# Three weight buffers instead of two in the expert blocks of a mixture-of-experts layer

## What is computed

```
g_w, g_idx = lax.top_k(jax.nn.softmax(g_logits, axis=-1), 1)
e_logits = e_logits[jnp.arange(t), g_idx[:, 0]]
e_w, e_idx = lax.top_k(jax.nn.softmax(e_logits, axis=-1), MOE_TOP_K)
...
def expert_block(args):
    xb, e = args
    h = jax.nn.silu(xb @ w_gate[e]) * (xb @ w_up[e])
    return h @ w_down[e]
```

## Time and profile before

| | us |
|---|---|
| median of 3 runs | 4761.02 (4743.81 to 4763.74) |
| profiled execution | 4764.29 |
| its span | 4762.6 |
| instructions executed in it | 56,977 |
| TensorE busy in the span | 3911.8 (82%) |
| VectorE, ScalarE, GpSimd busy | 1642.3, 706.3, 719.7 |
| stage experts, layer 0 | about 2931 to 3481, 32 blocks |
| stage experts, layer 1 | about 4124 to 4706, 34 blocks |

### The profile page before, as it was taken

One profiled execution on the slowest core, in us unless ns is written; L12 is line 12 of the kernel. 1 busy time (PEld: TensorE's weight loads), 2 busy tenths in 40 slices (PEclk: granted clock), 3 DMA queues, 4 the chain that ended last, 5 costly groups with the idle time before them and its releaser, 6 DMA issues. The chain is left out here.

```text
span 4762.6 us, 56977 instructions
## 1 busy us (share of the span) xinstructions
PE 3911.8 (82%) x23207; PEld 2625.4 (55%) x23207; DVE 1642.3 (34%) x3018; ACT 706.3 (15%) x1502; POOL 719.7 (15%) x595
## 2 busy tenths in 40 slices
PE   4989978999898878999899895877749977577773
PEld 2578855784446756864458743444427755344442
DVE  6667735530365653211341512000031143300003
ACT  2211211010222222100211500000010122000000
POOL 1123303330110213420100101000010033100001
PEclk9999978999899988999899896998969977699987
DMA  3221313623121012221221026999932100599995
GB/s 124 64 80 53 111 49 133 212 98 110 39 68 36 2 50 80 84 89 53 67 77 36 1 80 244 392 396 397 393 127 71 53 1 27 232 396 397 399 396 225
DMA packets 242989, 707.37 MB, mean 149 GB/s; under 512 B 22140, under 2 KB 117828, under 8 KB 192100
## 3 DMA queue, kind: packets, MB, share of 16 engines
q1 hardware_dynamic: 223060, 660.99, 37.5%
q10 hardware_dynamic: 15120, 26.76, 1.6%
q0 software_dynamic: 4608, 16.78, 0.9%
HBM read 667.24 MB, written 37.24 MB: 148 GB/s over the span
## 5 line engine op out<-in xcount | busy, mean ns | idle before, releaser
L3037 PE MATMUL experts_pg<-moe_wg,experts_xt 128*64 128x256 f32 x4224 | 529.4, 414 | 142.3 <-DMA moe_wg<-in_moe_w_up 127.8
L3037 PEld LDWEIGHTS experts_pg<-moe_wg,experts_xt 128*64 128x64 f32 x4224 | 334.5, 150 | 320.2 <-issue 178.0
L465 PE MATMUL ffn_out_y<-ffn_out_ring,ffn_h 128*128 128x512 f32 x704 | 308.8, 601 | 20.8 <-DMA ffn_out_ring<-in_ffn_w_out 20.8
L3052 PE MATMUL experts_py<-moe_wd,experts_ht 128*64 128x512 f32 x1056 | 256.4, 629 | 41.6 <-DVE experts_ht L3104 24.2
L86 PE MATMUL att_proj_ps<-att_proj_ring,ut 128*128 128x512 f32 x576 | 250.0, 597 | 15.6 <-DMA att_proj_ring<-in_attn_w_qkv 15.6
L3102 DVE TENSOR_TENSOR experts_h<-experts_hs,experts_pg 128x256 f32<-128x256 f32 x66 | 27.8, 421 | 659.2 <-ACT experts_hs L3071 659.2
L465 PEld LDWEIGHTS ffn_out_y<-ffn_out_ring,ffn_h 128*128 128x128 f32 x704 | 135.3, 193 | 190.5 <-issue 169.0
L562 PE MATMUL ffn_in_seven<-ffn_in_seven_t,ffn_in_seven_s 128*128 128x256 f32 x1056 | 238.4, 383 | 0.0
L86 PEld LDWEIGHTS att_proj_ps<-att_proj_ring,ut 128*128 128x128 f32 x576 | 177.5, 308 | 87.8 <-DMA att_proj_ring<-in_attn_w_qkv 16.0
L562 PEld LDWEIGHTS ffn_in_seven<-ffn_in_seven_t,ffn_in_seven_s 128*128 128x128 f32 x1056 | 204.0, 193 | 29.1
L562 PE MATMUL ffn_in_seven<-ut,ffn_in_ring 128*128 128x256 f32 x704 | 181.8, 404 | 19.1 <-DMA ffn_in_ring<-in_ffn_w_in 19.1
(11 more groups left out here) (651 smaller groups left out, 6294.0 us busy)
## 6 DMA issues: line engine op xcount, KB each, us to landing
moe_wg<-in_moe_w_gate SPq DMA_DIRECT2D x66, 2048.0 KB, 20.6
moe_wg<-in_moe_w_up SPq DMA_DIRECT2D x66, 2048.0 KB, 25.2
moe_wd<-in_moe_w_down SPq DMA_DIRECT2D x66, 2048.0 KB, 26.2
ffn_in_ring<-in_ffn_w_in SPq DMA_DIRECT2D x44, 1024.0 KB, 5.8
ffn_in_ada_ring<-in_ada_w SPq DMA_DIRECT2D x28, 1024.0 KB, 7.6
ffn_out_ring<-in_ffn_w_out SPq DMA_DIRECT2D x22, 1024.0 KB, 5.0
ssd_proj_ring<-in_ssd_w_in SPq DMA_DIRECT2D x20, 1024.0 KB, 5.3
att_proj_ring<-in_attn_w_qkv SPq DMA_DIRECT2D x9, 2048.0 KB, 7.9
```

Source lines behind the costliest of these rows:

```text
L465: last = nc.tensor.matmul(y[:, tt, half, :], h[:, kk, tt * P:(tt + 1) * P], ring[:, n % RING, q, half * BANK:(half + 1) * BANK], start=(kk ...
L3037: last = nc.tensor.matmul(pg[ch * SLOTS:(ch + 1) * SLOTS, b, side, 0:HH], xt[:, b, kk % MQ, kk // MQ, :], wg[:, b, side, kk, ch * HH:(ch + ...
L3052: last = nc.tensor.matmul(py[half * SLOTS:(half + 1) * SLOTS, b, :], ht[:, b, kk % HM, kk // HM, :], wd[:, b, kk, half * HALF:(half + 1) * ...
```

## The change

The weight buffers, and with them the buffers of a block's rows (`xg`), become three, taken by block modulo 3. They live in a stage of their own, `weights`, which encloses `route` and `experts` and ends before `merge`. `route` issues the weights of three blocks. In `experts` the first 30 blocks (PLAIN) are written out on every engine; only blocks from 30 on run in the loop over pairs, which takes buffers 0 and 1 and waits for block i-2 as before. In the written-out part a load waits for block n-3, and the expert is a constant, since block n of the first 32 belongs to expert n. The rows of blocks 0, 1 and 2 are issued by ScalarE at the beginning of `experts`, those of block 3 on by SyncE ahead of the same block's weights. Results, hidden values and PSUM stay in two buffers.

The diff without the lines that only gained indentation:

```
+WSLOTS, PLAIN = 3, FIRST - 2
...
-        wg, wd = outer.sb("wg", [P, 2, 2, DK, HID]), outer.sb("wd", [P, 2, HK, D])
-        gu_in, d_in = ([outer.sem(f"{n}{b}") for b in range(2)] for n in ("gu_in", "d_in"))
+        weights = Stage(nc, f"moe_w{l}")
+        wg, wd = weights.sb("wg", [P, WSLOTS, 2, DK, HID]), weights.sb("wd", [P, WSLOTS, HK, D])
+        gu_in, d_in = ([weights.sem(f"{n}{b}") for b in range(WSLOTS)] for n in ("gu_in", "d_in"))
...
+        with weights:
...
-                    for b in range(2):
+                        for b in range(WSLOTS):
                             load_gate_up(sp, slice(b, b + 1), b)
                             load_down(sp, slice(b, b + 1), b)
...
-            xg, yb = st.sb("xg", [P, 2, HALF]), st.sb("yb", [P, 2, HALF])
+                xg, yb = st.sb("xg", [P, WSLOTS, HALF]), st.sb("yb", [P, 2, HALF])
...
+                        for n in range(WSLOTS, PLAIN):
+                            load_rows(n, n % WSLOTS, n - WSLOTS + 1)
+                            sp.wait_ge(s["gu_made"], n - WSLOTS + 1)
+                            load_gate_up(sp, slice(n, n + 1), n % WSLOTS)
+                            sp.wait_ge(s["y_made"], n - WSLOTS + 1)
+                            load_down(sp, slice(n, n + 1), n % WSLOTS)
+                        with sp.Fori(PLAIN // 2, more + 1) as it:
+                            for b in range(2):
+                                i = 2 * it + b
+                                e = sp.value_load(info[0:1, bass.ds(i, 1)], min_val=0, max_val=E - 1)
+                                load_rows(i, b, i - 1)
                                 sp.wait_ge(s["gu_made"], i - 1)
                                 load_gate_up(sp, bass.ds(e, 1), b)
                                 sp.wait_ge(s["y_made"], i - 1)
                                 load_down(sp, bass.ds(e, 1), b)
...
-                    one(0, 0, 0, True)
-
-                    one(1, 1, 0, True)
-                    with pe.Fori(1, more + 1) as it:
+                        for n in range(PLAIN):
+                            one(n, n % 2, n % WSLOTS, n // WSLOTS, n < 2)
+                        with pe.Fori(PLAIN // 2, more + 1) as it:
                             for b in range(2):
-                            one(2 * it + b, b, it)
+                                one(2 * it + b, b, b, it - PLAIN // 2 + PLAIN // WSLOTS)
...
+                        for n in range(WSLOTS):
+                            r0 = act.value_load(info[0:1, n + B:n + B + 1], min_val=0, max_val=ASSIGN + SLOTS)
+                            for half in range(2):
+                                act.dma_start(xg[half * SLOTS:(half + 1) * SLOTS, n, :],
+                                              x_rows[bass.ds(r0, SLOTS), half * HALF:(half + 1) * HALF]).then_inc(x_in[n], 16)
```

512 lines of the change are left out of this document (252 added, 260 removed).

## The result

The change makes the kernel slower by a quarter of a per cent: 4770.16 us median of 20 runs against 4757.1, ratio 1.0025, 95% interval 1.0013 to 1.0037, so 6 to 18 us. The prediction was 4756, with no change that can be told. Its own bound for "no change" holds, its sign and its range do not.

A forecast was written before the change was run, and what follows sets the result against it. It took DMA bandwidth to bound the experts stage. Per layer -15.8 - 0.7 + 12.0 + 0.4 + 1.6 = -2.5 us, -5 us for two, gave 4756 us; the 8-in-10 range was 4732 to 4768.

The forecast's parts named there:

- bound for "no change": Whole kernel: a measurement tells about 0.5% (23.8 us) from no change; chance of staying within, 0.80.
- the bound: Experts stage: DMA bandwidth limits it, not late issue; engines' share 1.01 in both layers, 17.4 us a block.
- the scatter: End of route: sharing engines with the prefetch, it and all behind it come 12 us late a layer; bounds 0 to 12.9.
- the third block: Weights prefetched in route: takes off 15.8 us plus 0.7 us of rows, 16.5 us a layer.
- rival 1: Route: the scatter is served first and ends on time; 14.5 us gained a layer, 4732 us; chance 0.12.
- rival 3: DMA streams: mixed HBM reads and writes disturb each other, 3 us more a layer, 4762 us; chance 0.06.
- The extra stage: The new weights stage: one more semaphore clearing and one more barrier, 0.4 us a layer.
- Rows from ScalarE at nothing: Start of experts: issuing rows of blocks 0 to 2 from ScalarE costs nothing, at most 1.3 us a layer late.
- the written-out code: Experts: 6400 more instructions, 0.4 MB a layer of instruction traffic, cost 1.6 us a layer; lower bound 0.
- rival 2: Experts: TensorE starves for instruction pages at 7.3 us each, 139 us a layer partly hidden, near 4950 us; chance 0.06.
- the forecast's upper edge: Whole kernel: top of 4748 to 4761 us, given for a scatter late by 8 to 13 us; chance 0.66.
- none, the share is 1.01, so no reserve: Experts: engines already at full rate, so deeper buffers only fill idle time; pace stays 17.4 us a block.

The follow-up runs named there:

- after: The changed kernel as first measured and profiled, against the kernel before: 4770.16 us, ratio 1.0025.
- e4: The changed kernel run once more, nothing altered, against the kernel before: 4769.88 us, ratio 1.0014.
- the two before: The two profiles of the unchanged kernel, the original and a repeat: 4757.1 us for the original; 4757.1 us and ratio 0.9991 for the repeat.
- e12: The loop of six of e6 with two weight buffers instead of three, no third block in route: 4748.5 us, ratio 0.999 to the kernel before.
- e6: The changed kernel, three buffers, with blocks 6 to 29 in a loop over six on every engine: 4735.06 us, ratio 0.995 to the kernel before.
- e10: From e6, SyncE, ScalarE and VectorE written out, TensorE kept in the loop of six: 4747.84 us, ratio 0.9979 to the kernel before.
- e3: The changed kernel with the rows of blocks 0 to 2 issued by SyncE instead of ScalarE: 4768.05 us, ratio 1.0012 to the kernel before.
- e1: The changed kernel with the third block's weights issued in experts after block 0's rows landed, not in route: 4758.18 us, against 4762.4 of the kernel before.
- e5: The kernel before, two buffers, with only TensorE's first 30 blocks written out: 4770.92 us, ratio 1.002.
- e2: The changed kernel with two buffers instead of three, blocks still written out: 4773.64 us, ratio 1.0028 to the kernel before.
- the loop of six: Form of the code: six block copies ahead, then a loop over six for blocks 6 to 29; put into the changed kernel it measured 4735.06 us.
- e9: From e6, TensorE alone written out again for its 30 blocks: 4765.71 us, ratio 1.0014 to the kernel before.
- e14: From e12, TensorE alone back in the loop over pairs: 4762.14 us, ratio 1.0008 to the kernel before.
- e11: From e6, TensorE's blocks 0 to 17 written out, then two rounds of the loop of six: 4761.54 us, ratio 1.0015 to the kernel before.
- e15: From e12, GpSimd runs 80 written-out memsets beside each of 30 blocks, on a buffer nobody reads: 4792.7 us, ratio 1.0072 to the kernel before.
- e16: From e6, the third block's weights issued in route only after the scatter has landed: 4728.46 us, ratio 0.995 to the kernel before.
- e7: From e6, the third block's weights issued after block 0's rows landed, not in route: 4731.79 us, ratio 0.9941 to the kernel before.

## Why the prediction was wrong, step by step

**Right: the bound, the scatter, the third block.** Traffic is what the stage has to work off. The scatter pays for the prefetch: the first transposes are 11.1 and 11.7 us later (mean of after and e4 against mean of the two before) for the forecast 12.0. So rival 1 is out, and rival 3 is not needed. The third buffer itself takes 14.6 us off the stream, for 16.5. The extra stage costs 0.4 and 0.6 us, for 0.4, from the last block to merge. Scatter and third buffer together are worth 4.3 us a layer where the prediction had 4.5: e12 to e6 is -4.5 and -8.3, e12 to e10 -4.7 and +0.4. That the mean comes out so close is luck in part, with a spread of 9. Rows from ScalarE at nothing: right (e3).

The Trainium skill (DMA: Bandwidth & Descriptors, "Issuing engines are not separate DMA queues") says that the DMAs of all issuers run on the same 16 engines and interleave. e1 and the row of 420 GB/s above agree: weights and scatter together fill one set of engines.

**Wrong: "the written-out code", 1.6 us a layer.** This is the term of the sum that failed. The prediction took a page's bytes and its packets' share of 16 engines. The form costs 6 us a layer against the loop over pairs (e5, e2: 12.1 and 11.6 us for two) and 13 us against the loop of six (1050 against 1024). Those 4 to 5 us more, with the 2 us less of the third buffer, turn the forecast -2.5 us a layer into +3.5.

The number of pages was right: 38 more of TensorE's for the two layers, where the prediction had 19 a layer. Their price was not. Against the loop of six it is 1.0 to 1.2 us a page, which is about what one page occupies one DMA engine for, and not a sixteenth of it. Against the loop over pairs it is only 0.3 (12.1 us for 38 in e5), because that loop has a cost of its own. It is not rival 2: TensorE does not starve, its first blocks follow each other in 14.3 to 14.4 us with all code new, and what it waits for is weights (59.6 us).

One slip in the sums changes nothing: for a scatter 13 us late they give 4758, where the forecast's upper edge says 4761.

**Wrong: "none, the share is 1.01, so no reserve".** I wrote that a full share leaves nothing to gain but idle time, and that I would be wrong altogether if it hid a reserve. It did, though not one that a third buffer opens. e12 has the same two buffers, the same bytes of weights and the same share, and streams 399 GB/s for 394.

**The account**, per layer: scatter +11.4; third buffer -14.6; the loop over pairs gone -6.4; written out against loop of six +13; extra stage +0.5. Sum +3.9, measured (mean of after and e4 against mean of the two before) +3.4 and +3.6. The three middle terms are steps of one chain from before to after, by e12 and the loop of six with three buffers, so they add up whatever they are; e5 and e2 test the two of the code from outside, 6.0 and 5.8 for 6.6. Two layers are 7 us; the medians say 13, with an interval from 6, and in e4 7.

**What is shown and what is argued.** That the form of TensorE's code alone, with the same work and the same weights, makes a saturated stream longer or shorter is shown by e5, e9 and e14. That it does so through its instruction pages is argued: the dose of e11 and the pages of e15 speak for it, and e14, slower with fewer pages, says that it is not the whole. That some DMA engines end later than others is shown by the ends of the streams. That all pages pass through one or a few engines, which then fall behind, is argued; it would fit 1.1 us for a page of 16 KB, but the rows don't name single engines, it leaves the lower rate in the middle of the stream unexplained, and an 8 KB page, 0.3 us long, cost as much in e15. Open as well is why TensorE's loop over pairs costs 7 us a layer: e14 ends its stream with the same signs (0.44 and then 0.56 of share in the last microseconds), and it has only 146 pages of TensorE's, as few as the kernel before.

The Trainium skill (Runtime: NRT & Kernel Launch, "Instruction fetch mechanics") calls the crossing of a page mostly hidden, and full unrolling the form that kernels prefer where they can. For the fetching engine this case agrees: TensorE keeps its 14.3 us a block, and GpSimd's 80 memsets in e15 take 2.7 us or less in every block. For the stage it does not: written out, the same blocks stream 13 us a layer slower than in the loop of six.

## What to carry to other kernels

In a stage that the DMA engines bound, ask of each prefetch what it stands in front of: here the scatter that ends the stage before took back eleven of fifteen microseconds. With the same load issued after it, the third buffer kept 8 to 11 us a layer (e16 and e7 against e12), where ahead of it the mean was 4. Unrolled code is not free in such a stage, and neither is the shortest loop: a loop over six blocks beat both 30 written out and a loop over two, so try more than one length. And compare GB/s over like stretches, never the busy share alone: 389 and 399 GB/s both read 1.02.

## Not expected of the hardware

An engine that runs written-out code nobody waits for made the kernel 0.7% slower than the kernel before (34 us in the medians), and the streams 49 us longer than without it. It added 37 instruction pages; that they alone did it is likely and not shown. The loop over six blocks on TensorE streamed 7 us a layer faster than the loop over two, with the same work (e12 against e14).
